# A two-block network kernel: the first block's in-projection, state space and attention in a new written-out order, its loads and its tail rearranged

## The chip, the cores and the metric

The kernel runs on one core of a Trainium2 chip. A core has five engines that work side by side and meet through semaphores: TensorE (PE, matrix products into the banks of PSUM), VectorE (DVE), ScalarE (ACT), GpSimd (POOL) and SyncE (SP, which here issues nearly all DMAs). Each engine takes its instructions strictly in the order in which they are written; a wait holds everything behind it on that engine. The metric is the device time of one execution in microseconds (us), lower is better.

## The reference

256 tokens of width 1024 go through one mixed block (the first) and two further layers. Only the first block's front half is touched by the change, so the rest is cut.

```python
def first_block(x, ...):
    u = rmsnorm(h, norm_mix[l])
    proj = u @ w_in[l]                                   # 1024 -> 2048
    u_ssm, q, k, v = jnp.split(proj, [D_SSM, D_SSM + D_ATTN, D_SSM + 2 * D_ATTN], axis=-1)
    y_ssm = s5_branch(u_ssm, A_re[l], A_im[l], log_dt[l], B_re[l], B_im[l], C_re[l], C_im[l],
                      D_skip[l], w_glu[l], b_glu[l])
    y_attn = stick_breaking_attention(q, k, v)           # 8 heads of 64
    gates = jax.nn.sigmoid((u @ w_gate[l] + b_gate[l]))  # 1024 -> 2048
    g_ssm, g_attn = jnp.split(gates, 2, axis=-1)
    merged = g_ssm * (y_ssm @ w_up_ssm[l]) + g_attn * (y_attn @ w_up_attn[l])
    h = h + merged @ w_out[l]
    hid = jax.nn.relu(rmsnorm(h, norm_mlp[l]) @ w_ff1[l])
    h = h + (hid * hid) @ w_ff2[l]

def s5_branch(...):    # 32 groups, 64 complex states each
    a_bar = jnp.exp(lam * dt);  b_bar = ((a_bar - 1.0) / lam) * B
    bu = b_bar @ u;  states = associative_scan(a_bar, bu)
    y = Re(C @ states) + D_skip * u
    y = jax.nn.gelu(y);  y = y * jax.nn.sigmoid(y @ w_glu + b_glu)

def stick_breaking_attention(q, k, v):
    z = (q @ k) * scale                                  # keys before the query only
    log_fail = log_sigmoid(-z);  after = cumsum from the right, without itself
    w = exp(log_sigmoid(z) + after);  out = w @ v
```

## The kernel before

**Slabs.** Every weight matrix is cut into slabs of 128 x 2048 words (1 MB), counted from 0 in `plan()`: 0 to 7 are the in-projection (two for the state space's input, two each for q, k and v), 8 to 15 the gates, 16 glu, 17 to 20 the up-projections, 21 to 24 the out-projection. There are three slots. A slab's way is: SP loads it into `raw` (L386) once VectorE has split the slab that was there; ScalarE rounds it into `wh` (`act_round`, L405), once PE has used the slot's former slab; VectorE makes the rest `wl` = raw - wh (`dve_split`, L412); PE multiplies three times, high by high, high by low, low by high (`mm3`, L445). A slab takes 48 such matmuls of 256 columns. Its result stands in bank 4 or 5 (slab's parity) until ScalarE evicts it (L1436 and L1440 to the SBUF tiles `us`, `qT`, `kT`, `v_tok`; L1445 with tanh for the gates), which gives `lin_free`.

**Start.** x comes in two token halves; `big_dve` and `big_act` make the norm, `big_pe` turns it (L688, with dummy products on zeros, `keep_clock`, L821, between and behind the halves), ScalarE scales it (L722), VectorE makes the two parts `uh` and `ul` (`big_parts`, L783 and L784), on which slab 0 waits. `b1_pe_start` turns small vectors (L1068, L1070), `b1_pe_vec2` those of the later layers (L1075), `b1_pe_params` the state-space factors (L1160, L1163).

**State space.** 16 tiles of 128 states. For each, `pe_bu` makes the input products in bank 0 or 1 (L1203, L1204: 32 rows of contraction, fp32), VectorE turns them by the phase, scans them and makes four products with sine and cosine (`dve_state`, L1228 to L1240, into `prod[s % 2]`), and `pe_y` multiplies these with four factor tiles (L1214) into 32 of the 128 rows of bank 3. So four tiles fill the bank, and `dve_y` (L1245) takes it. The phases come in four groups of four tiles: angles, rounded off, then sine and cosine on ScalarE (`act_phase`, L1193 to L1195). VectorE makes the angles of groups 0 and 1 (`dve_phase`, L1170 to L1173), GpSimd those of 2 and 3 (`pool_phase`, L1180 to L1185).

**Attention.** For each of 8 heads: scores (`pe_z`, L1260, L1261), softplus on ScalarE (`act_softplus`, L1291 to L1294, with table loads), sum and mask on GpSimd (L1045, L1034), suffix product on PE (`pe_tri`, L1267 to L1271), exp on ScalarE (`act_weights`, L1300), weighted sum on PE (`pe_av`, L1281, L1282). There is one buffer each for the softplus (`at_sp`) and the weights (`at_w`), and two banks of scores.

**What sets the order.** A loop over 16 steps g, one slab each, on PE, VectorE and ScalarE. The table `tiles_at` says which state tiles VectorE takes at a step; `pe_bu` of its first tile comes at the end of the step before, `pe_y` a step later; head h starts at step 8 + h:

```python
tiles_at = {5: [0], 6: [1], 7: [2, 3], 8: [4, 5], 9: [6, 7], 10: [8, 9], 11: [10, 11], 12: [12], 13: [13],
            14: [14, 15]}
PHASES_AT = {1: [0, 1], 5: [2], 11: [3]}
```

**Tail.** After the last head come gelu on ScalarE, its two parts, glu on PE (bank 0), a sigmoid, the product with y, its two parts, then the four up-projection slabs in the order attention, state space, attention, state space, each gated by VectorE (L1396), the sums, and the out-projection, whose end lets the next norm start.

Of the kernel before, what the change touches and what calls it, by code (L numbers as in the profile page):

```python
# [14 lines left out]
P = 128  # L15
# [60 lines left out]
KC1, KC2 = 8, 10  # L76
# [26 lines left out]
def plan():  # L103
# [25 lines left out]
    for n in range(8):  # L129
        add("gate1", n)  # L130
    mark("glu")
    add("glu", 0)
    mark("up1")
    for n, w in enumerate(("up_attn", "up_ssm", "up_attn", "up_ssm")):
        add(w, n // 2)
# [52 lines left out]
def hybrid_ssm_attention_kernel(nc, a, out):  # L188
# [14 lines left out]
    with ExitStack() as ctx:  # L203
# [27 lines left out]
        gates = sb("gates", [P, 2 * KD, T])  # L231
        shared = sb("shared", [P, 4096])
# [442 lines left out]
        def big_pe(pe, j):  # L675

            for tt in range(NTT):
                if tt == 1:
                    keep_clock(pe, KC1, CLOCK_BANK[j])
# [189 lines left out]
        rows_in = flat(act_out)  # L869
        b_nat = [gflat[:, 2048 + 256 * i:2304 + 256 * i].rearrange("p (s c) -> p s c", c=16) for i in range(2)]  # L870
# [11 lines left out]
        def phase(i, which):  # L882

            buf, at = ((shared, 0), (shared, 2048), (gflat, 2048), (shared, 0))[i]
            return buf[:, at + which * 1024:at + which * 1024 + 1024].rearrange("p (j t) -> p j t", j=4)
        prod = [small[:, i * 1024:(i + 1) * 1024].rearrange("p (a t) -> p a t", a=4) for i in range(2)]
        ATT = 3 * P
# [8 lines left out]
         ph_later, zeroed, gn_in, gn_t, vec2_in, vec2_t, w2_in, cd_in) = mk(  # L896
# [3 lines left out]
            "glu_y", "glu_h", "glu_l", "pair_read", "merged_sum", "merged_h", "merged_l", "ph_later", "zeroed", "gn_in", "gn_t", "vec2_in", "vec2_t", "w2_in",  # L900
            "cd_in")


        tiles_at = {5: [0], 6: [1], 7: [2, 3], 8: [4, 5], 9: [6, 7], 10: [8, 9], 11: [10, 11], 12: [12], 13: [13],
                    14: [14, 15]}
        PHASES_AT = {1: [0, 1], 5: [2], 11: [3]}
        NSTEP = 16
# [52 lines left out]
        def ssm_loads(sp):  # L960
            for i, nm in enumerate(("B_re", "B_im")):
                sp.dma_start(b_nat[i], a[nm][0].rearrange("(s g) p c -> (g p) s c", g=2)).then_inc(ssm_in, 16)
# [3 lines left out]
            sp.dma_start(steps_t[:, :], a["shape_tables"][:, 4 * T + 2 * P:]).then_inc(ssm_in, 16)  # L966

        def later_vectors(sp):

            for l in range(LAYERS):  # L970
                for name, r0 in ROW2.items():
# [1228 lines left out]
```

## Time and profile before

| | |
|---|---|
| median of 3 runs | 1687.04 us (1685.98 to 1690.28) |
| the profiled execution, its own time | 1686.85 us |
| its span, mean granted TensorE clock | 1685.1 us, 0.988 |
| PE busy | 1622.0 us (96%) |
| DVE, ACT, POOL busy | 1111.7 us (66%), 828.3 us (49%), 48.5 us (3%) |
| chain that ended last, by engine | PE 87%, DVE 8%, ACT 2%, SPq 1%, issue 1% |
| DMA | 264.53 MB, mean 157 GB/s |

"Busy" of PE counts overlapping matmuls once, with modelled ends; PE can be busy and yet slow, when the granted clock is below 1. The chain is followed back from the last instruction, at each step to what released it. Busy time of an engine off this chain costs nothing by itself.

### The profile page before, as it was taken

The page shows a single profiled execution, that of the slowest core. Times are in us where ns is not written, and L with a number is a line of the kernel's source. Part 1 is how long each engine was busy: PE and PEld are TensorE (multiplying, and loading weights), DVE is VectorE, ACT ScalarE, POOL GpSimd, SP SyncE. Part 2 cuts the span into 40 slices and gives each one's busy share as a digit, 9 for nine tenths or more (in the row PEclk, how much of TensorE's full clock was granted, in tenths as well). Part 3 has the DMA queues.
Part 4 walks back from the last instruction along what each step waited for, and adds up shares of the span by engine and source line. Part 5 has one row for each costly group of instructions (what it writes and reads, how often), then busy time and mean ns, then how long its engine had stood idle before and what let it go on. Part 6 is the DMA issues. An engine that isn't in the chain of part 4 may idle for free.

```text
span 1685.1 us, 24642 instructions
## 1 busy us (share of the span) xinstructions
PE 1622.0 (96%) x9690; PEld 1386.1 (82%) x9690; DVE 1111.7 (66%) x1480; ACT 828.3 (49%) x1077; POOL 48.5 (3%) x58
## 2 busy tenths in 40 slices
PE   5999899999999999999999999999999999999997
PEld 5876797888788888887888888788889877978886
DVE  5976766666766568865576655856577765666566
ACT  5545745343454346655454434634355655454443
POOL 1321100000000000000000000000000000000001
PEclk8999999999999999999999999999999999999999
DMA  7521243655655655532345556555664512454652
GB/s 206 153 72 51 101 143 122 197 184 189 215 175 174 199 199 147 178 101 76 126 150 175 181 192 208 168 173 188 211 193 132 175 51 101 150 171 155 207 190 100
DMA packets 206812, 264.53 MB, mean 157 GB/s; under 512 B 14106, under 2 KB 176276, under 8 KB 206740
## 3 DMA queue, kind: packets, MB, share of 16 engines
q1 hardware_dynamic: 206548, 263.50, 48.5%
q8 instruction: 49, 0.80, 0.2%
q14 instruction: 23, 0.19, 0.0%
q10 hardware_dynamic: 192, 0.04, 0.0%
HBM read 262.47 MB, written 1.05 MB: 156 GB/s over the span
## 4 chain that ended last, share of the span: by engine, by line
PE 87%; DVE 8%; ACT 2%; SPq 1%; issue 1%; DMA 0%; ACTq 0%; DVEq 0%
PE bank L445 41%; PE bank L479 21%; PE bank L483 11%; DVE wl L412 3%; PE bank L1621 2%; PE bank L1648 2%; PE bank L1214 1%; PE bank L1634 1%; ACT wh L405 1%; PE bank L688 1%; PE bank L821 1%; DVE wl L431 1%; PE bank L1649 1%; PE bank L1203 1%; DVE norm_small L740 1%
## 5 line engine op out<-in xcount | busy, mean ns | idle before, releaser
L412 DVE TENSOR_TENSOR wl<-raw,wh 128x2048 fp32r<-128x2048 f32 (+2 forms) x228 | 510.6, 2244 | 113.1 <-ACT wh L405 110.0
L405 ACT CAST wh<-raw 128x2048 fp32r<-128x2048 f32 (+3 forms) x235 | 437.6, 1866 | 90.3 <-PE bank L445 80.5
L479 PE MATMUL bank<-u_parts,wh 128*128 128x512 f32 x1664 | 424.1, 392 | 1.5 <-DVE u_parts L784 1.0
L479 PEld LDWEIGHTS bank<-u_parts,wh 128*128 128x128 f32 x1664 | 302.9, 188 | 59.6 <-issue 2.0
L445 PE MATMUL bank<-u_parts,wh 128*128 128x256 f32 (+1 forms) x1344 | 258.3, 293 | 9.0 <-ACT tmp L1436 7.1
L483 PEld LDWEIGHTS bank<-u_parts,wl 128*128 128x128 f32 x1664 | 231.2, 190 | 15.4
L483 PE MATMUL bank<-u_parts,wl 128*128 128x256 f32 x1664 | 243.1, 282 | 0.0
L445 PEld LDWEIGHTS bank<-u_parts,wh 128*128 128x128 f32 (+1 forms) x1344 | 212.9, 194 | 13.7 <-ACT tmp L1436 7.3
L445 PE MATMUL bank<-u_parts,wl 128*128 128x256 f32 (+1 forms) x672 | 192.6, 287 | 0.0
L445 PE MATMUL bank<-wh,hh 128*128 128x512 f32 x448 | 179.4, 400 | 7.1 <-DVE wl L412 5.1
L445 PE MATMUL bank<-wl,hh 128*128 128x512 f32 x448 | 175.6, 392 | 0.0
L445 PE MATMUL bank<-wh,hl 128*128 128x512 f32 x448 | 175.1, 391 | 0.0
L624 DVE TENSOR_TENSOR gates<-gates,bank 128x512 f32<-128x512 f32 x44 | 30.2, 687 | 189.3 <-ACT gates L588 189.3
L588 ACT COPY gates<-bank 128x512 f32<-128x512 f32 x44 | 25.8, 586 | 248.6 <-PE bank L483 248.6
L592 ACT COPY gates<-bank 128x512 f32<-128x512 f32 x60 | 35.2, 587 | 193.9 <-PE bank L483 193.9
L445 PEld LDWEIGHTS bank<-u_parts,wl 128*128 128x128 f32 (+1 forms) x672 | 130.4, 194 | 0.0
L445 PEld LDWEIGHTS bank<-wh,hh 128*128 128x128 f32 x448 | 84.5, 189 | 28.7 <-DVE wl L412 5.9
L445 PEld LDWEIGHTS bank<-wh,hl 128*128 128x128 f32 x448 | 84.5, 189 | 18.2
L445 PEld LDWEIGHTS bank<-wl,hh 128*128 128x128 f32 x448 | 84.5, 189 | 15.6
L445 PE MATMUL bank<-wh,u_parts 128*128 128x512 f32 (+1 forms) x320 | 83.8, 348 | 0.0
L613 DVE TENSOR_TENSOR gates<-gates,bank 128x512 f32<-128x512 f32 x60 | 41.2, 687 | 63.0 <-ACT gates L592 63.0
L445 PE MATMUL bank<-bh,wh 128*128 128x256 f32 x208 | 60.2, 289 | 6.9 <-DVE bl L1498 5.2
(340 smaller groups left out, 2030.5 us busy)
## 6 DMA issues: line engine op xcount, KB each, us to landing
raw<-ffn_wg SPq DMA_DIRECT2D x44, 1024.0 KB, 5.8
raw<-ffn_wu SPq DMA_DIRECT2D x44, 1024.0 KB, 5.4
raw<-ffn_wd SPq DMA_DIRECT2D x44, 1024.0 KB, 5.0
raw<-w_ff SPq DMA_DIRECT2D x32, 1024.0 KB, 5.2
raw<-w_in SPq DMA_DIRECT2D x28, 1024.0 KB, 5.5
raw<-w_out SPq DMA_DIRECT2D x12, 1024.0 KB, 5.0
raw<-w_gate SPq DMA_DIRECT2D x8, 1024.0 KB, 5.6
raw<-w_in SPq DMA_DIRECT2D x16, 512.0 KB, 5.3
```

The source lines that it names most:

```text
L405: ins = act.copy(dst, src)
L412: ins = dve.tensor_tensor(dst, src, upper.bitcast(F32), ALU.subtract)
L431: ins = dve.tensor_tensor(wl[:, slot, c], raw[:, slot, c], wh[:, slot, c].bitcast(F32), ALU.subtract)
L445: mm = pe.matmul(o, w, x, start=start and n == 0, stop=stop and n == 2, skip_group_check=True)
L479: return pe.matmul(two(bank[b + f]), slab_view(wh, slot, KD, WCOLS)[:, k, f * P:(f + 1) * P], u_parts[:, k, :, :], start=k == 0, stop=Fals ...
L483: return pe.matmul(bank[b + f][:, 0:T], slab_view(wl, slot, KD, WCOLS)[:, k, f * P:(f + 1) * P], uh[:, k, :], start=False, stop=k == KD - ...
L588: act.copy(up_z, halves(6)[1]).then_inc(up_half_out, 1)
L592: act.copy(gate_z, halves(4)[1]).then_inc(gate_half, 1)
L613: dve.tensor_tensor(gate_z, gate_z, halves(4)[0], ALU.add).then_inc(gate_sum, 1)
L624: dve.tensor_tensor(up_z, up_z, halves(6)[0], ALU.add).then_inc(up_sum, 1)
L1621: pe.matmul(b[:, c], q_(slice(tt * P, (tt + 1) * P)), k_(slice(0, (tt + 1) * P)), start=tt == 0, stop=True, skip_group_check=True)
L1648: pe.matmul(bank[6][r, 0:T], v_(0), pt[:, 0:T], start=first, stop=True, skip_group_check=True)
```

## The change

- **Order.** The loop is gone. `b1_pe`, `b1_act` and `b1_dve` are written out, step by step. PE takes most slabs in two halves (`pe_slab1(pe, g, half)`) with one to four small products between them. The state tiles start earlier (`pe_bu(0)` between the halves of slab 4, where it stood behind the whole slab 4), and so do the heads (scores of head 0 ahead of slab 6).
- **Output products in pairs.** `prod` has four buffers, two of them in a new tile `late_prod`; `pe_y(pe, s0)` takes tiles s0 and s0 + 1 and alternates between them, one factor after the other.
- **Phases.** ScalarE makes the angles (`act_turns`, 16 products with a column), VectorE rounds them off for all four groups; GpSimd has none. ScalarE also takes over the copies of the diagonal factors (`b1_act_diag`) and of the output factors (`b1_act_turned`). The phases of groups 2 and 3 stand in the buffers of 0 and 1.
- **Loads.** On SP, slabs 0 to 2 come first, then the steps, C and B_re, slab 3, B_im, slab 4; the vectors of the later layers in three parts ahead of slabs 6, 7 and 8, the small weights ahead of slab 12.
- **Start.** 20 dummy products before the first transposes, `b1_pe_start` between the two token halves in place of 8 dummies.
- **Tail.** Slab 16 is now the first attention up-projection, 17 glu (banks 2 and 3), 18 the second attention one, 19 and 20 those of the state space. `dve_up` is split into `dve_gate` and `dve_merge`.
- The DMA scratch is set to 1024, which makes room for `late_prod`.

```diff
-KC1, KC2 = 8, 10
+KC0, KC1, KC2 = 20, 8, 10
...
-                if n == 1:
-                    ssm_loads(sp)
-                if n == 2:
-                    later_vectors(sp)
+                if n == 3:
+                    steps_and_c(sp)
+                    b_load(sp, 0)
+                if n == 4:
+                    b_load(sp, 1)
+                if n in (6, 7, 8):
+                    later_vectors(sp, n - 6)
+                if n == 12:
+                    cmp_weights(sp)
                 sp_slab(sp, n)
...
+        def pe_y(pe, s0):
+            if s0 % 4 == 0 and s0 >= 4:
+                pe.wait_ge(y_taken, s0 // 4)
+            pe.wait_ge(prod_done, s0 + 2)
             for n, (c, q) in enumerate(((0, 0), (1, 3), (2, 2), (2, 1))):
-                mm = pe.matmul(bank[3][32 * j:32 * j + 32, 0:T], c_t[c][:, s, :], p[:, q, :], start=n == 0, stop=n == 3)
-            mm.then_inc(y_done, 1)
+                for s in (s0, s0 + 1):
+                    j = s % 4
+                    mm = pe.matmul(bank[3][32 * j:32 * j + 32, 0:T], c_t[c][:, s, :], prod[s % 4][:, q, :], start=n == 0, stop=n == 3)
+                    if n == 3:
+                        mm.then_inc(y_done, 1)
...
-            if s >= 2:
-                dve.wait_ge(y_done, s - 1)
-            p = prod[s % 2]
+            if s >= 4:
+                dve.wait_ge(y_done, s - 3)
+            p = prod[s % 4]
...
+        def act_turns(act, i):
+            s = phase(i, 1)
+            if i < 2:
+                act.wait_ge(ssm_in, 16 * 7)
+            else:
+                act.wait_ge(prod_done, 4 * (i - 1))
+            for j in range(4):
+                ins = act.activation(s[:, j, :], steps_t[:, :], ACT.Identity, scale=col(TURNS)[:, 4 * i + j:4 * i + j + 1])
+            ins.then_inc(ph_in, 1)
...
+            pe_slab1(pe, 3)
+            b1_pe_params(pe)
+            pe_slab1(pe, 4, 0)
+            pe_bu(pe, 0)
+            pe_slab1(pe, 4, 1)
+            b1_pe_vec2(pe)
+            pe_slab1(pe, 5, 0)
+            pe_bu(pe, 1)
+            pe_slab1(pe, 5, 1)
+            pe_bu(pe, 2)
+            pe_z(pe, 0)
+            pe_slab1(pe, 6, 0)
...
+            pe_slab1(pe, 9, 0)
+            pe_bu(pe, 6)
+            pe_y(pe, 2)
+            pe_tri(pe, 1)
+            pe_slab1(pe, 9, 1)
+            pe_bu(pe, 7)
+            pe_av(pe, 1)
+            pe_z(pe, 2)
...
+            pe_slab1(pe, 15, 1)
+            pe_av(pe, 7)
+            pe_y(pe, 14)
+            pe.wait_ge(o_taken, 4)
+            pe.wait_ge(bu_free, ST)
+            lin_pe(pe, N_UP1, 0, None, KS, 512, 4, *upper(KS))
             pe.wait_ge(gelu_l, 1)
-            lin_pe(pe, N_GLU, 0, None, KS, DS, 4, lambda k: bh[:, k, :], lambda k: bl[:, k, :])
+            pe.wait_ge(w_exp, HEADS)
+            lin_pe(pe, N_GLU, 2, None, KS, DS, 4, *upper(0))
```

SP, from its first DMA on. `raw<-w_in` is a slab, `res<-x` a token half, the others state-space parameters and vectors. Before:

```order
L985 DMA res<-x 128x1024 x2
L386 DMA raw<-w_in 128x8x256
L962 DMA gates<-B_re 128x16x16
L962 DMA gates<-B_im 128x16x16
L965 DMA hid<-C_re 128x4x64 x2
L965 DMA stat<-C_im 128x4x64 x2
L966 DMA steps_t<-shape_tables 128x256
L386 DMA raw<-w_in 128x8x256
L977 DMA act_out<-ln_f_g 8x128
```

And now:

```order
L989 DMA res<-x 128x1024 x2
L389 DMA raw<-w_in 128x8x256 x3
L963 DMA steps_t<-shape_tables 128x256
L966 DMA hid<-C_re 128x4x64 x2
L966 DMA stat<-C_im 128x4x64 x2
L969 DMA gates<-B_re 128x16x16
L389 DMA raw<-w_in 128x8x256
L969 DMA gates<-B_im 128x16x16
L389 DMA raw<-w_in 128x8x256 x2
```

Three slabs stand ahead of the parameters, where one did; the vectors have gone behind slab 5.

PE, between the slabs of step 8 and step 9 before, around the output products of tiles 2 and 3 (L1214; L1203 and L1204 are `pe_bu`):

```order
L1203 MATMUL bank<-tmp,tables 128x256
L1204 MATMUL bank<-tmp,tables 128x256
L1267 MATMUL bank<-small,suffix 128x256
L1268 MATMUL bank<-small,minus1 128x128
L1269 MATMUL bank<-small,suffix 128x128
L1271 MATMUL bank<-earlier,identb 128x128 x2
L1214 MATMUL bank<-small,tables 32x256 x8
L1203 MATMUL bank<-tmp,tables 128x256
L1204 MATMUL bank<-tmp,tables 128x256
L1260 MATMUL bank<-sq 128x256
L1261 MATMUL bank<-sq 128x128
```

Now, between the halves of slab 9, the same two tiles (L1221 is `pe_bu`, L1234 `pe_y`, L1290 to L1294 `pe_tri`):

```order
L1221 MATMUL bank<-tmp,tables 128x256 x2
L1234 MATMUL bank<-late_prod,tables 32x256 x8
L1290 MATMUL bank<-small,suffix 128x256
L1291 MATMUL bank<-small,minus1 128x128
L1292 MATMUL bank<-small,suffix 128x128
L1294 MATMUL bank<-earlier,identb 128x128 x2
```

Before, two state products and a head's scores stood with them, and the second `pe_bu` needed a bank that VectorE frees after `dve_y`; now it is one group less, and the next `pe_bu` stands behind half a slab.

VectorE, at the end of the heads (L1245 is `dve_y`, L1308 the last head's low part, L412 a split, L1498 gelu's low part, L1396 the gating). Before:

```order
L1308 TENSOR_TENSOR bl<-bank,bh 128x256
L412 TENSOR_TENSOR wl<-raw,wh 128x2048
L1245 SCALAR_TENSOR_TENSOR tmp<-tmp,vec1,bank 128x256
L1308 TENSOR_TENSOR bl<-bank,bh 128x256
L1498 TENSOR_TENSOR bl<-tmp,bh 128x1024
L412 TENSOR_TENSOR wl<-raw,wh 128x2048
L1501 TENSOR_TENSOR tmp<-tmp,small 128x1024
```

And now (L1334, L1266, L415, L1695, L1496 in the same roles):

```order
L415 TENSOR_TENSOR wl<-raw,wh 128x2048
L1334 TENSOR_TENSOR bl<-bank,bh 128x256
L1266 SCALAR_TENSOR_TENSOR tmp<-tmp,vec1,bank 128x256
L415 TENSOR_TENSOR wl<-raw,wh 128x2048 x2
L1695 TENSOR_TENSOR bl<-tmp,bh 128x1024
L1496 SCALAR_TENSOR_TENSOR small<-gates,bank 128x512 x2
L1698 TENSOR_TENSOR tmp<-tmp,small 128x1024
```

Two splits now stand between `dve_y` and gelu's low part; the second of them is of slab 18, which ScalarE rounds behind gelu.

## Rows read from the trace of the kernel before

**Rows 1.** The page, part 1: busy us, share of span, instructions.
```profile
PE 1622.0 (96%) x9690; PEld 1386.1 (82%) x9690; DVE 1111.7 (66%) x1480; ACT 828.3 (49%) x1077; POOL 48.5 (3%) x58
```
**Rows 2.** Busy by stretch: length, engines (instructions), granted clock, DMA share, GB/s.
```profile
6.00:8.00 2.00, 0.00 (x0) 0.00 (x0) 1.60 (x5) 1.73 (x4) 1.18 (x4) 1.00 1.09 376
...
60.00:204.00 144.00, 135.05 (x851) 108.08 (x850) 108.43 (x149) 79.62 (x100) 31.63 (x24) 0.95 0.28 90
```
**Rows 3.** PE in order of time: start, busy, instruction [idle before, releaser].
```profile
16.75 0.47 PE L445 MATMUL bank<-u_parts,wh 128*128 128x256 f32 x2
...
36.62 0.80 PE L445 MATMUL bank<-u_parts,wh 128*128 128x256 f32 x2 [7.10 <-ACT tmp L1436]
...
51.95 1.09 PE L1160 MATMUL bank<-ident,gates 128*128 128x128 f32 x8 [1.00 <-DVE gates L1139]
...
103.15 0.69 PE L1203 MATMUL bank<-tmp,tables 32*128 32x256 f32 x2 [3.97 <-DVE hid L1229]
...
265.60 1.24 PE L688 MATMUL bank<-ident,sq 128*128 128x128 f32 x8 [1.05 <-ACT sq L706]
```
**Rows 4.** VectorE and ScalarE in order of time, the start.
```profile
11.52 2.29 DVE L412 TENSOR_TENSOR wl<-raw,wh 128x2048 fp32r<-128x2048 f32 x1 [0.25 <-ACT wh L405]
15.85 0.29 DVE L783 CAST u_parts<-tmp 128x256 fp32r<-128x256 f32 x1 [2.04 <-ACT tmp L722]
...
15.34 2.49 ACT L722 ACTIVATE tmp<-bank,vec 128x256 f32<-128x256 f32 x6 [3.86 <-PE bank L688]
...
32.25 1.90 ACT L405 CAST wh<-raw 128x2048 fp32r<-128x2048 f32 x1 [9.75 <-DMA raw<-w_in]
```
**Rows 5.** SP's queue in order of time: start, us issuing, DMAs.
```profile
2.81 6.00 SPq L962 DMA_DIRECT2D gates<-B_im  x1
...
26.57 28.04 SPq L386 DMA_DIRECT2D raw<-w_in  x6
```
**Rows 6.** The chain that ended last, in order of time: start, us, piece.
```profile
61.66 5.94 PE bank L445 x48
...
74.61 1.84 PE bank L1214 x8
...
96.44 2.75 PE bank L1214 x16
...
99.61 2.28 DVE wl L412
...
106.05 8.04 PE bank L445 x48
...
140.51 7.90 PE bank L445 x48
```
**Rows 7.** L1214 on PE by tenths of a microsecond (in brackets: records in flight).
```profile
97.40:97.50 0.10, 0.10 (x5) 1.00 0.00 0
...
75.00:75.10 0.10, 0.10 (x2) 1.00 0.00 0
```
**Rows 8.** The chain again, from the last head to glu.
```profile
202.42 0.50 ACT small L1300
...
203.61 0.23 PE bank L1282 x2
...
204.26 1.28 ACT L1456
...
207.71 1.24 DVE bl L1498
...
209.00 7.84 PE bank L445 x48
```
**Rows 9.** VectorE in order of time: first state tile, and two tiles in a row.
```profile
65.43 0.69 DVE L1228 TENSOR_TENSOR act_out<-bank,shared 128x512 f32<-128x512 f32 x1
...
101.81 0.68 DVE L1228 TENSOR_TENSOR act_out<-bank,shared 128x512 f32<-128x512 f32 x1
...
106.62 0.69 DVE L1228 TENSOR_TENSOR act_out<-bank,shared 128x512 f32<-128x512 f32 x1
```

More of the change, by code:

```diff
@@ L130, in plan @@
         add("gate1", n)
+    mark("up1")
+    add("up_attn", 0)
     mark("glu")
     add("glu", 0)
[L133 to L135 removed]
+    add("up_attn", 1)
+    add("up_ssm", 0)
+    add("up_ssm", 1)
     mark("out1")
@@ L1277, in pe_av @@
             pe.wait_ge(w_exp, h + 1)
+            if h == 0:
+                for b_ in range(2):
+                    pe.wait_ge(lin_free[b_], 4)
             if h % 2 == 0 and j >= 1:
@@ new lines, in dve_up, with act_evict @@
+        def dve_up(dve, n0, r, q):
+            p = q // 2
+            dve_gate(dve, n0 + q, 2 * (q % 2), "AB"[q % 2], p, merged[:, 4 * p:4 * p + 4, :] if q % 2 == 0 else gated)
+            if q % 2:
+                dve_merge(dve, r, p, q + 1)
+        def act_evict(act, g):
+            wait_used(act, N_IN1 + g)
+            b = bank[4 + g % 2]
+            if g < 2:
+                act.copy(us[:, 2 * g:2 * g + 2, :], two(b)).then_inc(lin_free[g % 2], 1)
+            elif g < 8:
+                o = (qT[:, 2 * (g - 2):2 * (g - 2) + 2, :] if g < 4 else kT[:, 2 * (g - 4):2 * (g - 4) + 2, :] if g < 6
+                     else v_tok[:, :, (g - 6) * WCOLS:(g - 5) * WCOLS])
+                act.activation(o, two(b), ACT.Copy, scale=SCALE_N if g < 4 else 1.0).then_inc(lin_free[g % 2], 1)
+            else:
+                for f in range(2):
+                    k = 2 * (g - 8) + f
+                    ins = act.activation(gates[:, k, :], b[:, f * T:(f + 1) * T], ACT.Tanh, scale=0.5, bias=half_b[:, k:k + 1])
+                ins.then_inc(lin_free[g % 2], 1)
@@ new lines, in b1_dve @@
+            dve_state(dve, 5)
+            dve_split(dve, 10)
+            dve_state(dve, 6)
+            dve_y(dve, 0)
+            dve_split(dve, 11)
+            dve_phase(dve, 2)
+            dve_split(dve, 12)
+            dve_state(dve, 7)
+            dve_state(dve, 8)
+            dve_state(dve, 9)
+            dve_o(dve, 0)
+            dve_split(dve, 13)
+            dve_split(dve, 14)
+            dve_state(dve, 10)
+            dve_y(dve, 1)
+            dve_phase(dve, 3)
+            dve_state(dve, 11)
@@ L1495, in b1_dve @@
+            dve_state(dve, 12)
+            dve_o(dve, 1)
+            dve_split(dve, 15)
+            dve_state(dve, 13)
+            dve_y(dve, 2)
+            dve_state(dve, 14)
+            dve_o(dve, 2)
+            dve_state(dve, 15)
+            dve_split(dve, N_UP1)
+            dve_o(dve, 3)
             dve_y(dve, 3)
-            dve_o(dve, 3)
+            dve_split(dve, N_GLU)
+            dve_split(dve, N_UP1 + 2)
+            for b in range(2):
+                dve.wait_ge(lin_free[b], 8)
```

475 lines of the change are left out of this document (277 added, 198 removed).

## The prediction, made before the changed kernel had run

> **What bounds the kernel now.** I read the page first. TensorE (PE) is busy 96% of the span [rows 1], so time can come only from where it idles, runs at its low clock, or does dearer work than needed. The changed stage is the first 265 us; nothing after it is edited, so its end (the last matmul of the out-projection at 264.6, ahead of the 1.05 us wait at 265.60 [rows 3]) is the mark: what that moves, the kernel moves. The busy time of 60 to 204 us shows that something is lost in the middle of it: granted clock 0.95 and 135 of 144 us busy [rows 2]. Then I follow the start in order of time [rows 3 to 5], and the chain of work that ended last [rows 6, 8]. Four losses are seen there.
>
> A: PE idles 7.10 us ahead of its third slab (36.62), because ScalarE waited 9.75 us for that slab's load [rows 3, 4]; SP issued it at 26.57, behind seven parameter DMAs and 32 vector and small-weight DMAs [rows 5]. The slab then starts at the low clock: its first pair of matmuls is busy 0.80 us, where slab 0's took 0.47 at 16.75 [rows 3], and its first nine groups of three take 0.64 us each instead of 0.36, some 2.2 us of loss until 42.3.
> B: PE waits 3.97 us at 103.15 [rows 3] for VectorE, which does `dve_y`, then a split of 2.28 us, and only then frees the bank of the next state tile; afterwards the clock is low, and the slab takes 8.04 us against 5.94. A second such wait ends at 136.65, with a slab of 7.90 [rows 6].
> C: a tile's four output products take 1.84 us, two tiles in a row 2.75 [rows 6].
> D: from 203.84 to 209.00 PE waits for gelu, and the glu slab takes 7.84 [rows 8].
>
> **The change, part by part,** against this execution (1686.85 us, its span 1685.1; the median of the runs shown is 1687.04, so the two agree).
>
> 1. Start. Twenty dummies come before anything else, and the vector transposes move between the two token halves. Before, ScalarE gets its first turned half at 15.34 [rows 4]. Now the vector transposes wait for the vectors as before (10.2), but the first token half is turned by then and the second follows near 11.7. VectorE, whose first split ends at 13.81 [rows 4], becomes the bound: its parts start at 13.85 instead of 15.85, slab 0 at 14.7 instead of 16.75. Gain 2.0 us.
>
> 2. Loads. SP issues slabs 0, 1 and 2 at once, then steps, C and B_re, slab 3, B_im, slab 4. x and three slabs are 4 MB; at the 376 GB/s of 6 to 8 us [rows 2] they are in by about 14 us. Splits 1 and 2 follow the parts on VectorE, 2.25 us each: to 21.4 and 23.7. PE starts slab 1 at 21.4 and slab 2 at 27.3, where it was 36.62: 9.3 earlier, 2.0 of it item 1's. The low clock of 36.6 to 42.3 goes too, 2.2 us. Gain 7.3 + 2.2 = 9.5. What is late next is ScalarE's queue: slab 1's eviction at 27.9, eight products for phases 0 and 1 (3.3 us, at the 0.415 us of a 128x256 row: six in 2.49 [rows 4]), rounds of 1.9, the diagonal copies until 37.1, and PE wants them at 39.2; the output factors are copied at 43.4, wanted at 44.2; slab 3's eviction at 47.4, wanted at 48.5. These are margins of 2.1, 0.8 and 1.1 us. PE's wait of 1.00 at the parameter transposes [rows 3] goes, with two shorter ones of 0.6 together: gain 1.6; for the thin margins I take 1.0 back.
>
> 3. Loss B. The first state tile starts on VectorE near 46.7 instead of 65.43, and a tile takes it 4.7 us (101.81 to 106.62 with a gap) [rows 9]; from there it is one to four tiles ahead of PE. I walked the queues with durations of this trace (half a slab 2.97, state product 1.06, output pair 2.0, scores 0.84, suffix product 1.15, weighted sum 0.80): bu(7) is wanted at 94 and its bank free at 89, bu(14) wanted at 153 and free at 146. The suffix products wait for ScalarE's softplus and GpSimd; the least margins are 1.7 us, at heads 3 and 7. So both stalls go, 3.97 each, and the slow groups behind them (slab 2.1, state product, scores and weighted sum 1.0): gain 2 x 7.07 = 14.1. Phases off GpSimd: GpSimd is waited for less, no gain on the path. ScalarE takes 16 products (6.6 us), some copies (4 us) and one more table load (1.28 [rows 8]); it is then busy some 111 of 155 us, hidden by PE's work as long as the order fits, and 1.28 to 2 us for each place where it doesn't.
>
> 4. Loss C. Six pairs at 2.75 and four single tiles at 1.84 are 23.9 us. In a pair up to 5 records are in flight together, in a single tile 2 [rows 7]: the second tile's column strip works beside the first. Interleaved, each strip has its 8 records at 0.23, so 1.84 and one step, say 2.0; eight pairs 16.0, gain 7.9. Bounds: 1.84 (gain 9.2), and no more overlap than now (2.75, 22.0, gain 1.9). I take 2.0, as the stretch with both strips runs each at its full rate.
> The Trainium skill, page "TensorE: Matmul & The Clock Gate", section "Part 3: Packing small matmuls", says that a weight load overlaps a running matmul only where the row groups differ; these products all use all 128 rows. By that rule the interleaved records would take turns, which is the third rival's time. The five records in flight speak against it.
>
> 5. Slabs in halves. 48 matmuls at the 0.12 us of an undisturbed slab are 5.76; with a group of another shape behind it a slab takes 5.94 [rows 6], so a return costs 0.18. There are 8 more returns: loss 1.5.
> The Trainium skill, page "TensorEngine Tiling (Array Packing)", section "Key Properties", says that changing the tiling mode drains the engine, which speaks against cutting slabs. The 0.18 us is what the trace shows of it.
>
> 6. Last heads. Two short waits for ScalarE around 202.42 [rows 8] go, as the weighted sums have slack now: gain 1.0.
>
> 7. Tail. Before, from 203.84 to 264.6 are 60.7 us. Now the first up slab (5.94) runs while gelu is made. The last output pair ends near 169.5. ScalarE has the glu slab's round and the table load until 172, gelu and its copy until 174.1 (204.26 to 207.71 are 3.45 with the load [rows 8]), then the round of the third up slab until 176.0; VectorE stands at that slab's split, until 178.2, and only then makes gelu's low part, 1.24 [rows 8]: 179.5. PE is through the up slab at 175.5, so it still waits 4.0 us, and I charge 2.0 for the clock as behind the 3.97 us waits. glu ends at 187.4; three up slabs, the zeroing and the out-projection take 40.3: 227.7. That is 58.2 us, gain 2.5. Bounds: 0 if the wait is 6 us, 4.5 if the clock holds.
>
> Sum: 2.0 + 9.5 + 1.6 - 1.0 + 14.1 + 7.9 - 1.5 + 1.0 + 2.5 = 36.1, and 1686.85 - 36.1 = 1650.8. In one line: PE starts slab 0 at 14.7, has 154.6 us of work and waits to the last pair (169.3), and ends the stage near 227.7, 36.9 earlier, 35.9 with the margins' 1.0. I predict 1651.
>
> **Rivals.** First: the order fits worse than my walk, and two waits are long enough to drop the clock. One costs what loss B does, 7.1 us, two 14.2: 1665. For it: margins of 0.8 to 2.1 us at five places, ScalarE strictly in order. Against: VectorE's lead.
> Second: slab 2 is still late, as the queue doesn't deliver three slabs in a row at that rate, or slab 3, behind the small-element loads. The 9.5 stays away: 1660. For it: SP was held 6.00 us at B_im [rows 5]. Against: slabs 1 and 2 are ahead of those loads now.
> Third: the output records take turns. 16 at 0.23 are 3.7 a pair, 29.4 in all, 5.5 more than before instead of 7.9 less: 1664. With today's overlap only, 1657.
> Fourth, the other side: **the head chain becomes the bound.** One buffer each for the softplus and the weights ties a head's suffix product to ScalarE's place in line; where the new order puts rounds, phases and table loads ahead of a head's softplus, PE stops at that product. At 7.1 us a stop with its clock, the 36.1 are gone with the sixth of eight heads, and all eight cost 56.8: 1651 + 57 = 1708. Against: ScalarE is about 72% loaded.
> That the change doesn't do what it says: the phases' leaving GpSimd frees no PE time, which I already count at nothing.
>
> **How the numbers follow.** Forecast 1651, with 1645 to 1657 from the bounds of items 4 and 7: 0.60. First rival 0.18, second 0.07, third 0.11 (0.04 of it at 1664), fourth 0.03, something else 0.01. The range 1645 to 1666 takes in the second and third and most of the first's single and double stops; left out are the rest of the first (0.06), the fourth, and the forecast's own ends (0.08): 0.17. Faster by over 0.3% (about what a measurement of this kernel can tell from no change; below 1682) is every case but the fourth and a sliver: 0.96; within 0.3% 0.015, slower 0.025.
>
> **What would show it.** Slab 2 starting near 27; the first state tile on VectorE near 47; no PE wait for a state bank and a granted clock of 1.00 from 20 to 170; output pairs of 16 records in about 2.0 us, the last ending near 169; one wait of about 4 us before glu; the next norm's transposes near 229. Wrong would be: PE waits at suffix products (first, fourth), pairs over 2.7 us (third), a round that waits for a load (second).

## The result, and the profile after

The changed kernel takes 1650.93 us (median of 4 runs, 1650.58 to 1651.91), the kernel before 1687.3 us in the same session: a ratio of 0.9777, 95% interval 0.9765 to 0.9789. The forecast was 1651 with a range of 1645 to 1666. The profiled execution has a span of 1648.4 us where it was 1685.1. Its page: the span and part 1 [the counterparts of rows 1], and from part 2 the granted clock, in tenths, over 40 equal slices:

```profile
span 1648.4 us, 24663 instructions
PE 1608.8 (98%) x9702; PEld 1378.8 (84%) x9702; DVE 1107.4 (67%) x1466; ACT 839.5 (51%) x1104; POOL 25.6 (2%) x46
PEclk9999999999999999999999999999999999999998
```

PE's busy time hardly differs (1622.0 before): it idles less, and at the low clock it also counts as busy. What PE waited for from the start to 226 us, then stretches of that time with the columns of [rows 2]:

```profile
PE bank L826 <- POOL cvalid L1032: 4.9, 1, 4.9
PE bank L448 <- DVE bl L1695: 3.9, 1, 3.9
PE bank L448 <- DVE u_parts L789: 2.3, 1, 2.3
PE bank L448 <- DVE bl L1701: 0.2, 1, 0.2
```

```profile
15.00:19.00 4.00, 4.00 (x23) 4.00 (x22) 3.79 (x13) 3.43 (x6) 0.00 (x0) 0.57 1.03 151
19.00:23.00 4.00, 4.00 (x36) 4.00 (x35) 4.00 (x3) 3.20 (x3) 0.00 (x0) 1.00 1.08 280
...
177.00:183.00 6.00, 5.97 (x29) 5.97 (x30) 1.17 (x2) 0.00 (x0) 0.00 (x0) 0.53 0.46 174
...
20.00:170.00 150.00, 150.00 (x1101) 128.37 (x1100) 131.78 (x191) 112.74 (x151) 14.57 (x16) 1.00 0.40 121
```

From 20 to 170 us PE is busy all the time at the full clock; before, 60 to 204 us had 135 busy of 144 at 0.95 [rows 2]. The four losses of the prediction are answered one by one. A: the wait of 7.10 us ahead of the third slab [rows 3] is gone; PE goes through slabs 0 to 3 until the parameter transposes at 39.3. B: both state-bank waits are gone. C: the output pairs, in the chain of work that ended last (start, us, piece), where a pair of tiles took 2.75 and a single one 1.84 [rows 6]:

```profile
73.34 1.85 PE bank L1234 x16
...
157.77 1.85 PE bank L1234 x16
```

D: there is still one wait of 3.91 ahead of glu, and the clock is low behind it (0.53 from 177 to 183 us). PE's waits in order of time, then the chain around it [answers to rows 3 and 8]:

```profile
14.69 0.48 PE L448 MATMUL bank<-u_parts,wh 128*128 128x256 f32 x2 [2.25 <-DVE u_parts L789]
177.03 0.58 PE L448 MATMUL bank<-bh,wh 128*128 128x256 f32 x1 [3.91 <-DVE bl L1695]
192.40 0.38 PE L448 MATMUL bank<-bh,wh 128*128 128x256 f32 x1 [0.19 <-DVE bl L1701]
227.00 1.24 PE L693 MATMUL bank<-ident,sq 128*128 128x128 f32 x8 [1.04 <-ACT sq L711]
```

```profile
166.47 1.79 ACT wh L408
168.28 1.28 ACT L1613
169.57 1.07 ACT tmp L1613
...
171.62 1.91 ACT wh L408
173.55 0.06 DVE wl L415
...
175.76 1.23 DVE bl L1695
176.99 0.04 issue
177.03 8.47 PE bank L448 x48
```

ScalarE has gelu's high part ready near 171.7. VectorE stands at the split of slab 18 instead, for which ScalarE first rounds the slab, and comes to gelu's low part at 175.8. PE has been idle since 173.1. The mark that the prediction chose, the transposes of the next norm, moved from 265.60 [rows 3] to 227.00.

### The profile page after: what moved, and what is told of

The parts are those of the page before. It is cut to its first block, busy times and chain, and to the rows that moved or that the text cites. A ratio compares the mean times of both kernels' runs of the same rounds, so it can differ in the third digit from the quotient of the medians.

```text
span 1648.4 us, 24663 instructions
## 1 busy us (share of the span) xinstructions
PE 1608.8 (98%) x9702; PEld 1378.8 (84%) x9702; DVE 1107.4 (67%) x1466; ACT 839.5 (51%) x1104; POOL 25.6 (2%) x46
## 4 chain that ended last, share of the span: by engine, by line
PE 89%; DVE 7%; ACT 3%; issue 1%; DMA 0%; ACTq 0%; DVEq 0%
PE bank L448 43%; PE bank L482 21%; PE bank L486 11%; DVE wl L415 2%; PE bank L1822 2%; PE bank L1849 2%; ACT wh L408 1%; PE bank L1221 1%; PE bank L1835 1%; PE bank L693 1%; PE bank L1234 1%; DVE norm_small L745 1%; PE bank L826 1%; DVE wl L434 1%; PE bank L1850 1%
## 5 line engine op out<-in xcount | busy, mean ns | idle before, releaser
L415 DVE TENSOR_TENSOR wl<-raw,wh 128x2048 fp32r<-128x2048 f32 (+2 forms) x228 | 509.7, 2240 | 99.8 <-ACT wh L408 96.8
L448 PE MATMUL bank<-u_parts,wh 128*128 128x256 f32 (+1 forms) x1344 | 254.1, 290 | 3.1 <-DVE u_parts L789 2.3
L486 PEld LDWEIGHTS bank<-u_parts,wl 128*128 128x128 f32 x1664 | 231.2, 190 | 15.4
L448 PEld LDWEIGHTS bank<-u_parts,wh 128*128 128x128 f32 (+1 forms) x1344 | 208.6, 191 | 9.0 <-issue 4.7
```

The lines of the kernel that those rows point to most:

```text
L415: ins = dve.tensor_tensor(dst, src, upper.bitcast(F32), ALU.subtract)
L448: mm = pe.matmul(o, w, x, start=start and n == 0, stop=stop and n == 2, skip_group_check=True)
L486: return pe.matmul(bank[b + f][:, 0:T], slab_view(wl, slot, KD, WCOLS)[:, k, f * P:(f + 1) * P], uh[:, k, :], start=False, stop=k == KD - ...
```

## A thing to know before the experiments: the untouched rest is not constant

The mark moved by 38.6 us, the span only by 36.7. From the mark to the end the two kernels execute the same instructions with the same waits (one of them 0.3 us longer), in 1419.5 us before and 1421.4 after. Of these 1.9 us 1.5 lie in one stretch: from a norm's transposes to a wait of PE in the second block, 76.8 us before and 78.3 after. Inside it stand four rotary products of 32x32 by 512 columns in a row (L1936, eight records, 3.62 us), and here is what the granted clock does behind them, first before, then after:

```profile
704.00:707.00 3.00, 3.00 (x27) 1.51 (x26) 2.80 (x5) 0.33 (x1) 0.00 (x0) 1.00 1.09 373
707.00:710.00 3.00, 3.00 (x36) 2.68 (x34) 2.97 (x2) 1.19 (x2) 0.00 (x0) 1.00 0.75 232
```

```profile
665.00:668.00 3.00, 3.00 (x14) 1.19 (x13) 2.80 (x5) 0.82 (x1) 0.00 (x0) 0.88 1.07 368
668.00:671.00 3.00, 3.00 (x33) 3.00 (x31) 2.94 (x3) 0.00 (x0) 0.00 (x0) 0.55 0.89 281
```

There is a second such place. Some 179 us behind the mark PE waits 2.02 us in every kernel, and in 10 of the 14 executions below the clock is low right behind it, which costs 1.1 us (not in the runs 3, 5, 9 and 11). The two places together account for nearly all of the differences in the column "rest".

So the experiments are read by places inside the first 230 us, and the medians beside them. "Rest" is the span less the mark; ratios are to the kernel before in the same session (its medians: 1687.3, 1687.9 for the runs 1 to 4, 1688.7 for 5 to 8, 1689.6 for 9 to 12).

| run | median us | ratio, 95% | glu starts | mark | rest |
|---|---|---|---|---|---|
| before | 1687.3 | 1 | 209.00 | 265.60 | 1419.5 |
| changed kernel | 1650.93 | 0.9777 (0.9765 to 0.9789) | 177.03 | 227.00 | 1421.4 |
| 1 tile by tile | 1655.48 | 0.9803 (0.9786 to 0.9819) | 183.01 | 230.54 | 1422.8 |
| 2 loads late | 1660.09 | 0.9829 (0.9813 to 0.9846) | 188.86 | 237.89 | 1422.7 |
| 3 before, y step late | 1676.31 | 0.9931 (0.9914 to 0.9947) | 195.48 | 251.49 | 1421.5 |
| 4 gelu first | 1644.02 | 0.9735 (0.9719 to 0.9751) | no wait | 220.86 | 1423.1 |
| 5 tail filled | 1648.27 | 0.9755 (0.9739 to 0.9771) | 176.81 | 224.36 | 1421.5 |
| 6 start filled | 1650.26 | 0.9765 (0.9749 to 0.9782) | 176.87 | 225.91 | 1423.0 |
| 7 slabs whole | 1651.07 | 0.9774 (0.9758 to 0.9791) | 178.88 | 227.77 | 1419.7 |
| 8 phases on GpSimd | 1649.74 | 0.9766 (0.9749 to 0.9782) | 177.22 | 226.07 | 1419.6 |
| 9 rotary products spread | 1649.35 | 0.9764 (0.9751 to 0.9778) | 177.25 | 226.12 | 1420.1 |
| 10 three edits | 1643.55 | 0.9726 (0.9713 to 0.9740) | no wait | 220.20 | 1421.1 |
| 11 and five slabs whole | 1641.13 | 0.9716 (0.9703 to 0.9730) | no wait | 218.77 | 1420.1 |
| 12 no start dummies | 1651.43 | 0.9766 (0.9753 to 0.9779) | 176.79 | 226.55 | 1423.0 |

## Experiments

**1. The pairs, tile after tile.**

```diff
-            for n, (c, q) in enumerate(((0, 0), (1, 3), (2, 2), (2, 1))):
-                for s in (s0, s0 + 1):
+            for s in (s0, s0 + 1):
+                for n, (c, q) in enumerate(((0, 0), (1, 3), (2, 2), (2, 1))):
```

> The changed kernel, in which the eight output products of a pair are written tile after tile again (order of the two loops in pe_y exchanged); all else stays, the four product buffers and the places of the pairs too. Theory of item 4 (two column strips work beside each other only when their records alternate): each of the eight pairs goes from the 1.85 us of the changed kernel's trace back to about 2.75, +0.9 x 8 = +7.2, so about 1658, with no new wait. Rival (the strips overlap however they are ordered, and the gain of the pairs came from bringing two tiles together): 1651, pairs still at 1.85. Rival (pairs longer by 0.9 us push a later product past its slack): 1662 or more, with a wait of PE that the changed kernel doesn't have.

Measured: every pair takes 2.74, as expected, but the median is 1655.5 where 1658 was. Two rows of its chain, and its wait ahead of glu:

```profile
73.13 2.74 PE bank L1234 x16
...
162.88 2.74 PE bank L1234 x16
```

```profile
183.01 0.39 PE L448 MATMUL bank<-bh,wh 128*128 128x256 f32 x1 [3.02 <-DVE bl L1695]
```

So alternating the two column strips is worth 0.89 a pair, 7.1 in all (in the order of this run the second tile's records start only with the first tile's fifth of eight, at 73.95, and half of each tile runs alone), and bringing tiles into pairs the remaining 2.0 of the 9.1 (23.9 to 14.8). But the mark is only 3.5 later than the changed kernel's, and the ratio only 0.0026 (4.4 us) higher: PE reaches the gelu wait 6.9 later, the low part comes 6.0 later, the wait is 0.9 shorter, and behind it the clock doesn't fall (glu to slab 19 takes 12.9 us instead of 15.4). Slab 0 happened to run at the full clock too (slab 2 starts at 27.55 instead of 27.77). 7.1 - 0.9 - 2.4 - 0.2 = 3.6, and 3.5 are measured. So 3.3 of the pairs' 7.1 was lost again at the tail's wait in the profiled executions; 2.4 of it is the clock's part, which varies (run 5), and by the ratios 2.7 was lost.

**2. The old order of SP.**

```diff
-                if n == 3:
-                    steps_and_c(sp)
-                    b_load(sp, 0)
...
+                if n == 1:
+                    b_load(sp, 0)
+                    b_load(sp, 1)
+                    steps_and_c(sp)
+                if n == 2:
+                    for part in range(3):
+                        later_vectors(sp, part)
+                    cmp_weights(sp)
```

> The changed kernel with SP's order of before: slab 0, the seven parameter loads, slab 1, all 24 later vectors and the eight small weights, slab 2. All other engines keep the changed order. Theory of item 2: slab 2 starts near 36.6 us on PE instead of 27.9, PE sits idle some 7 to 9 us ahead of it and then runs some groups at the low clock (2.2 us by the trace of before): +9 to +11, so 1660 to 1662. Rival (the engines' new orders take the loads' place: the gain of the start came from the order of ScalarE and VectorE, not from the loads): within 2 us of 1651. Rival (the parameter path, which the early loads no longer feed late, becomes faster and gives part back): 1655 to 1658.

Measured: slab 1 starts 1.8 later (23.83, behind a new wait of 1.51 for VectorE's split), slab 2 at 37.22, and its first pair of matmuls runs at the low clock (0.77 us):

```profile
37.22 0.77 PE L448 MATMUL bank<-u_parts,wh 128*128 128x256 f32 x2 [7.37 <-ACT tmp L1521]
```

Slab 3, and glu too, start 11.8 later (45.36 instead of 33.53, 188.86 instead of 177.03); the mark is 10.9 later, as the clock's fall behind the tail's same wait of 3.91 cost 1.0 less in this execution; the ratio is 0.0052 (8.8 us) higher. One more wait appears, of 0.2 us at the start's vectors. The loads' place, and not the engines' new order, gives the start its gain; between slab 3 and glu nothing of it was given back.

**3. Loss B alone, in the kernel before.**

```diff
-                for s in tiles_at.get(g - 1, []):
-                    if s % 4 == 3 and s < ST - 1:
-                        dve_y(dve, s // 4)
                 if g >= 4:
                     dve_split(dve, n + 2)
                 for s in tiles_at.get(g, []):
                     dve_state(dve, s)
+                for s in tiles_at.get(g - 1, []):
+                    if s % 4 == 3 and s < ST - 1:
+                        dve_y(dve, s // 4)
```

> The kernel before with one edit: on VectorE the y step of the tiles of slab g-1 is written behind the split and the states of slab g instead of ahead of them, so that VectorE no longer stands at it while the next state tile's bank is waited for. Theory of loss B: both 3.97 us waits of PE for that bank go, and the low clock behind each (3.1) with them: 1687.3 - 14.1 = 1673. If only the waits go and the clock falls in any case: 1679. Rival (the order of VectorE only moves the wait: the split or the state's products are late next): 1683 to 1690, with PE waits at another product.

Measured: in place of the two 3.97 us waits there are two short ones, and the clock holds. PE in order of time, then 60 to 160 us of this kernel:

```profile
111.29 0.69 PE L1203 MATMUL bank<-tmp,tables 32*128 32x256 f32 x2 [0.25 <-DVE hid L1229]
125.94 0.69 PE L1203 MATMUL bank<-tmp,tables 32*128 32x256 f32 x2 [0.97 <-DVE hid L1229]
```

```profile
60.00:110.00 50.00, 50.00 (x340) 41.25 (x339) 43.85 (x56) 26.39 (x30) 19.33 (x11) 1.00 0.36 113
110.00:160.00 50.00, 48.53 (x318) 38.16 (x316) 44.82 (x64) 34.16 (x44) 9.80 (x9) 1.00 0.26 85
```

From slab 2 to glu PE needs 159.8 us instead of 172.4, 12.6 less: 6.7 of waits (7.94 less 1.22) and 5.9 of clock, 2.9 for each, where I charged 3.1. The median falls by 11.6, where 14.1 was expected. One moved step of 0.48 us gives nearly all of item 3; only the last 1.2 us of waits are left to the written-out order. The rival (the wait moves elsewhere) falls.

**4. Gelu's low part ahead of the split of slab 18** (changed kernel, VectorE).

```diff
             dve_split(dve, N_GLU)
-            dve_split(dve, N_UP1 + 2)
-            for b in range(2):
-                dve.wait_ge(lin_free[b], 8)
             dve.wait_ge(gelu_h, 1)
             dve.tensor_tensor(bl[:, 0:KS, :], us[:, :, :], bh[:, 0:KS, :].bitcast(F32), ALU.subtract).then_inc(gelu_l, 1)
+            dve_split(dve, N_UP1 + 2)
+            for b in range(2):
+                dve.wait_ge(lin_free[b], 8)
```

> The changed kernel with one edit: on VectorE the low part of gelu is written ahead of the split of slab 18 instead of behind it. ScalarE has gelu's high part ready at 171.7 in the changed kernel's trace, so the low part ends near 172.9, and PE is through the first up slab at 173.1. Theory of item 7: PE's wait of 3.9 us ahead of glu goes, and with it the low clock of 176 to 183 (about 2.5 us): 1651 - 6.4 = 1644.5. If the clock falls there in any case: 1647. Rival (the split of slab 18 or glu's own chain of sigmoid, product and parts is next, and takes it back): 1649 to 1651, with a PE wait at slab 18 or at slab 19.

Measured: the first up slab and glu are one piece of 96 matmuls in the chain, at 5.94 a slab:

```profile
167.47 11.88 PE bank L448 x96
179.35 0.02 issue
179.38 0.03 ACT small L1618
```

The mark is 6.1 earlier, the ratio 0.0042 (7.1 us) lower, with intervals apart: 1644.0 us. The cause of the tail's wait is shown: not gelu, but VectorE's place in line. The next wait, 0.20 for the gated product's low part, is the same as before.

**5. The same gap, filled.**

```diff
-            pe.wait_ge(gelu_l, 1)
             pe.wait_ge(w_exp, HEADS)
+            keep_clock(pe, 26, 7)
+            pe.wait_ge(gelu_l, 1)
```

> The changed kernel with 26 dummy products (128x256, 0.144 us each in the start's rows) into a free bank between the first up slab and the wait ahead of glu: 3.7 us of work in the 3.9 us gap, the wait itself stays. Theory (the gap costs its length plus a clock that falls because of it): only the low clock of 176 to 183 goes, glu's slab takes 5.9 instead of 8.5: 1651 - 2.4 = 1648.5. Rival (the clock falls there for another reason): 1651. Rival (the dummies run past the end of the wait): up to 1652.

Measured: glu starts at the same time, but the clock holds:

```profile
176.81 0.39 PE L448 MATMUL bank<-bh,wh 128*128 128x256 f32 x1 [0.81 <-DVE bl L1696]
189.75 0.39 PE L448 MATMUL bank<-bh,wh 128*128 128x256 f32 x1 [0.20 <-DVE bl L1702]
```

12.9 us between the two rows, and 15.4 in the changed kernel: the gap costs its 3.9 us and 2.4 of clock, and dummies save the second part. That is read from the traces; the intervals of the two ratios overlap. The seven executions that kept a wait of 3.6 us or more ahead of glu need 14.2 to 15.4, so the clock's part is 1.3 to 2.4. Behind waits of 3.02 and 0.81 it was nothing.

**6. The gap ahead of slab 0, filled** with `keep_clock(pe, 15, 5)` ahead of `pe_slab1(pe, 0)`.

> The changed kernel with 15 dummy products more just ahead of slab 0, in PE's 2.25 us gap from 12.4 to 14.7. Theory (the gap lowers the clock for slab 0, groups of three at 0.64 us from 15.6 to 18.7): slab 0 runs at the full clock, but it is fed by VectorE's parts, one in 0.66 us until 19.1, and slab 1's split ends at 21.4; slab 0 ends near 20.4 instead of 22.1, PE waits for slab 1 until 21.4: gain 0.7, 1650.2. Rival (the clock falls there whatever stands before): 1651. What would be larger than 1.5 us speaks against both.

Measured: no wait before slab 0, slab 1 at 21.75, behind a wait of 0.77 for VectorE's split:

```profile
21.75 0.50 PE L448 MATMUL bank<-u_parts,wh 128*128 128x256 f32 x2 [0.77 <-DVE wl L415]
```

That is 0.3 earlier than the changed kernel's 22.01, and 0.7 was expected: the bound is VectorE's split, as told, but it lets slab 1 start at 21.75 and not at 21.4. The median can't tell it. The low clock of 15 to 19 us costs only this much. It isn't in every execution: slab 0 ran at the full clock in the runs 1, 5 and 12, behind gaps of 1.29, 1.36 and 2.00 us, and at the low one behind gaps of 1.97 to 2.53 (runs 2, 4, 7, 8, 9 and the changed kernel).

**12. No dummies at the start** (the line `keep_clock(pe, KC0, 5)` taken out).

> The changed kernel without the 20 dummy products at the very start (4.86 to 9.1 us). The transposes of the first token half start when x is normalised, not when the dummies end, and VectorE's split of slab 0 (11.6 to 13.8) stands ahead of the parts in either case. If the dummies are there for the clock of the start: transposes at the low clock, slab 0 wholly at the low clock, up to 3 us more at slab 1, which VectorE's split (21.4) lets start no earlier: 1651 to 1653. If the clock is low in slab 0 anyway, as in the changed kernel's trace: 1651, no change.

Measured: the first transposes take 1.94 us, where they took 1.03. Their records start 0.21 us apart instead of 0.11, the step of a low clock; the trace has no record of the clock itself before 11.15 us, so that is worked out and not read:

```profile
7.92 1.94 PE L693 MATMUL bank<-ident,sq 128*128 128x128 f32 x8 [7.92 <-ACT sq L711]
14.91 0.48 PE L448 MATMUL bank<-u_parts,wh 128*128 128x256 f32 x2 [2.00 <-DVE u_parts L789]
```

Slab 0 starts within 0.22 of the changed kernel's all the same and ran at the full clock. The 20 dummies buy nothing that can be measured.

**7. All cut slabs whole** (the ten calls `pe_slab1(pe, g, 0)` become `pe_slab1(pe, g)`, the ten second halves go).

> The changed kernel with the ten cut slabs (4 to 6 and 9 to 15) whole again, each at the place of its first half; every other step of every engine keeps its order. Theory of item 5: each cut costs a return of 0.18 us (two halves take 3.06 and 2.92 in the changed kernel's trace, a whole slab 5.76 to 5.94), gain 10 x 0.15 = 1.5 if nothing is late; but what stood between the halves now comes 2.9 us later, and a state tile, a suffix product or an eviction that had less slack than that makes PE wait. If the halves are there for the waits, the loss is larger than 1.5: 1652 to 1660 with PE waits at state, score or suffix products. If they aren't needed: 1649.5.

Measured: 1651.07, no change, but for two reasons against each other. There are four new waits, 0.64, 0.86, 0.58 and 0.22 us, at the scores of heads 5 and 7, at the last weighted sum and at the first up slab. Behind the second one the clock falls:

```profile
150.56 0.70 PE L1283 MATMUL bank<-sq 64*128 64x256 f32 x2 [0.86 <-ACT small L1326]
```

```profile
150.00:154.00 4.00, 3.44 (x11) 2.28 (x12) 3.90 (x8) 3.39 (x6) 0.00 (x0) 0.66 0.00 0
154.00:158.00 4.00, 4.00 (x33) 3.99 (x32) 0.79 (x2) 2.87 (x5) 0.00 (x0) 0.91 0.00 0
```

Glu starts 1.85 later. So some of the cuts hold off the waits of the later heads. Together they pay for themselves and no more, as far as these medians tell.

**8. Phases 2 and 3 on GpSimd again.**

```diff
-            act_turns(act, 2)
-            act_turns(act, 3)
-            dve_phase(dve, 2)
-            dve_phase(dve, 3)
...
+                for i, step in {0: [(2, 0)], 1: [(2, 1), (2, 2)], 2: [(3, 0)], 3: [(3, 1)], 4: [(3, 2)]}.get(h, []):
+                    pool_phase(pool, i, step)
```

> The changed kernel with phases 2 and 3 on GpSimd again (products, rounding and subtraction, spread behind heads 0 to 4); ScalarE and VectorE lose those eight products and four rounding steps. Theory of item 3 (the phases are off the path, whoever does them): within 1.5 us of 1651, with VectorE's steps a little longer where GpSimd works beside it. Rival (GpSimd is slow at them, 13 us a phase by the trace of before, and its head steps come late, or phase 2 itself does): PE waits at suffix products or at state tile 8, and loses 4 to 14 us with the clock: 1655 to 1665.

Measured: 1649.74, glu at 177.22 (177.03), no new wait of PE. GpSimd's steps for the two phases, from the groups of instructions (busy us, mean ns):

```profile
L1209 POOL TENSOR_SCALAR shared<-steps_t,cols 128x256 f32<-128x256 f32 x8 | 8.4, 1070 | 10.5 <-DVE late_prod L1276 10.5
L1212 POOL TENSOR_SCALAR shared<-shared 128x1024 f32<-128x1024 f32 x2 | 7.6, 3820 | 0.0
L1214 POOL TENSOR_TENSOR shared<-shared 128x1024 f32<-128x1024 f32 x2 | 5.5, 2740 | 0.1
```

21.5 us of GpSimd's time, none of it on the path. Taking the phases off it, which the change does, is worth nothing by itself.

**9. The rotary products spread**, one ahead of the 48 small products that follow them and one behind each of the first three quarters of these, in both layers.

```diff
+                    if between is not None and k in (3, 7, 11):
+                        between((k + 1) // 4)
...
-            for b in range(4):
+            def rope_perm(b):
                 pe.wait_ge(m_read, 4 * l + b + 1)
                 pe.matmul(bank[b][HD:QK_M, :], perm_m[HD:QK_M, HD:QK_M], qm[HD:QK_M, 2 * b:2 * b + 2, :], start=True,
                           stop=True).then_inc(m_perm, 1)
+            rope_perm(0)
             pe.wait_ge(bank7_free, B7 * l + NROPE + 1)
-            cmp_hidden(1)
+            cmp_hidden(1, rope_perm)
```

> The changed kernel with one edit far behind the changed stage, in both layers of the second block: the four rotary products of 32x32 by 512 columns, which stand in a row in 3.6 us and use a sixteenth of the array, are spread through the 48 small products of the second compression slab (one ahead, one behind each quarter). What is to be explained: with the same instructions and the same waits, the time from the first transposes behind the changed stage to the end of the kernel is 1419.5 us in three executions and 1421.4 to 1423.0 in seven; all of the difference lies in the stretch of these products in each layer (76.8, 78.3 or 79.8 us), where the granted clock falls to 0.50 for some 3 or 6 us with PE busy throughout. Theory (four products in a row that use so little of the array lower the clock in some executions): spread, both stretches take 76.8, and the time from that mark to the end is 1419.5; the median falls by 1 to 2 us, 1649 to 1650. Rival (the clock falls there for another reason, the matmuls of 30 rows on either side among them): stretches of 78.3 or 79.8 are still found, and the median stays at 1651. Rival (a rotary step is late for VectorE now): the stretch takes longer without a low clock.

Measured: the clock holds.

```profile
664.00:668.00 4.00, 4.00 (x30) 1.73 (x28) 1.38 (x2) 0.00 (x0) 0.00 (x0) 1.00 1.09 361
668.00:672.00 4.00, 4.00 (x31) 3.21 (x31) 3.76 (x3) 3.00 (x4) 0.00 (x0) 1.00 0.15 47
```

With the products in a row, 12 of 22 such stretches (11 executions, two layers) took 78.2 to 78.3 or 79.7 to 79.8 us, the others 76.8; spread, all six (runs 9, 10 and 11) took 77.4 to 77.5. So the four in a row bring the falls about. Whether that is for their shape, as the theory has it, or for something else about them isn't separated here. The edit has a price that I had not foreseen, 0.65 us a stretch against an undisturbed 76.8, with more changes of shape on PE, and so it saves little: 1.0 on average less 0.65. Most of the 2.2 us by which run 9's ratio lies under the changed kernel's isn't from it, and the intervals overlap: the profiled execution's rest is 1.3 us shorter than the changed kernel's, and 1.1 of that is the fall at the second place, 179 us behind the mark, which it was spared. That the median came out as forecast is luck.

**10. The edits of 4, 6 and 9 together.**

> Three edits of the experiments together on the changed kernel: the low part of gelu ahead of the split of slab 18, the 15 dummies ahead of slab 0, the rotary products spread. From the medians of the runs so far: 1644.0 with the first, 0.5 to 0.7 for the second, 1 to 2 for the third, so 1642 (1640.5 to 1643.5). If the clock's falls at the start and in the second block are not tied to these places, 1644.

Measured 1643.55, just above the expected 1640.5 to 1643.5; the mark is 6.8 us earlier than the changed kernel's. The intervals of this run and of run 4 (0.9719 to 0.9751) overlap, so what the two other edits add to run 4's isn't told by the medians; in the profiled executions the mark is 0.7 earlier and the rest 1.9 shorter.

**11. And slabs 4, 5, 6, 9 and 10 whole.**

> As the kernel with the three edits, and slabs 4, 5, 6, 9 and 10 whole again, the ones ahead of which the run with all slabs whole showed no wait. Five returns of 0.15 to 0.18 us: 0.8 us less than the kernel with the three edits if no wait appears. If a wait appears that the later heads' order had hidden: same or longer.

Measured 1641.13: no wait appears, and the mark is 1.43 earlier than in run 10, where 0.8 was expected. In the chain, first of run 10 and then of run 11, the first half of slab 10 takes 3.06 (the second one too) and the whole slab 5.93:

```profile
95.21 3.06 PE bank L448 x24
```

```profile
93.95 5.93 PE bank L448 x48
```

Five cuts cost 0.3 us each. This is the fastest version, 0.6% under the changed kernel by the ratios (0.9716 and 0.9777, intervals apart).

## Why the prediction came out, point by point

The four losses, their causes and most of their prices were right. That the time was right within 0.1 us is partly luck: the stage ended 1.7 us earlier than I had it (225.96, not 227.7), and the rest took 1.9 us longer, by low clocks that I had not counted. **The step that failed** is the first paragraph's "what that moves, the kernel moves": the rest of the kernel varies between 1419.5 and 1423.1 us with the same instructions.

- Item 1, the start: slab 0 at 14.69, forecast 14.7. That it would run at the low clock was missed; PE reached slab 1 at 22.0 instead of 21.4. Run 6 gets 0.3 of it back.
- Item 2, the loads: slab 2 at 27.8, forecast 27.3; run 2 puts their worth at 11.8 at glu, where items of 9.5 and 1.6 less 1.0 stood. One term was summed too low: the third slab took 8.41 us before and 5.76 now, 2.65 and not the 2.2 charged for its low clock. The first state tile starts on VectorE at 47.15, forecast 46.7; the waits at the parameters are gone, and the margins held. The second rival (slab 2 or 3 late) was close for slab 3 alone: ScalarE waited 0.86 us for its load, VectorE 0.51 for that round, and PE for neither.
- Item 3, loss B: 14.1 forecast; run 3 gives 12.6 with 1.2 of waits left.
- Item 4, the pairs: 2.0 a pair taken, 1.85 measured, at the lower bound of 1.84; gain 9.1 instead of 7.9. The reason was right: the records start two by two, one of each strip, 0.007 us apart, and the twos follow each other at 0.216, the step at which a single tile's records follow too. The step for "one more record" was not needed. Four records are in flight at a time, first in the changed kernel; in run 1, where the first of two tiles runs alone, it is two [as rows 7]:

```profile
73.53:73.72 0.19, 0.19 (x4) 0.10 (x2) 1.00 0.09 9
```

```profile
73.50:73.60 0.10, 0.10 (x2) 0.09 (x1) 1.00 0.08 18
```

  The Trainium skill, page "TensorE: Matmul & The Clock Gate", section "Part 3: Packing small matmuls", lets a weight load overlap a running matmul only where the row groups differ. These all use 128 rows, each matmul record is busy 0.379 (with a modelled end), and the weight loads, 0.11 each, start just behind the start of a matmul record and not behind its end: this trace doesn't agree with the rule. The third rival falls by the 1.85 us alone.
- Item 5, the cuts: I charged 0.18 for each of eight; run 11 shows 0.3 for each of five. Mis-sized by the count and by the price.
- Item 6, the last heads: the trace of before shows one wait there, of 0.64 us, and none is left; 1.0 was forecast.
- Item 7, the tail: the wait was 3.91 (forecast 4.0), the place and the reason as told, and the clock's price 2.4 (forecast 2.0; it is 1.3 to 2.4 in other executions). What I missed is that the pairs' gain runs against this wait (run 1): items 4 and 7 aren't independent.
- The last pair starts at 165.2 and PE is free for the up slab at 167.1, 2.2 earlier than forecast; 1.2 of it are the pairs, the other 1.0 I didn't trace.
- First and fourth rival: no PE wait from 20 to 170 us. Run 7 shows that they weren't idle: with ten halves merged, waits at scores appear and one of them lowers the clock, but each costs 0.2 to 0.9 us and one fall of the clock, not 7.1.

## What to carry to other kernels

Where small matmuls write to different column strips, alternate the strips record by record; side by side in program order isn't enough (2.74 against 1.85 us). Before adding up gains, look for the next wait that another engine sets: up to half of the pairs' gain vanished at the gelu wait, and one VectorE instruction moved past a split was worth more (7 us). And time a small edit by marks inside the trace: far from the edit the same instructions took up to 3.5 us more or less.

## What the runs showed of the hardware

The granted clock fell to its lower level (0.50, that is 1.2 of 2.4 GHz) with PE busy throughout, behind 3.6 us of 32x32 products, in 12 of 22 passes through them, and in none of 6 once they were spread. The Trainium skill, page "TensorE: Matmul & The Clock Gate", section "HAM oscillation — how this bites in real kernels", lays such falls to gaps in which PE is idle; here there was no gap, so the rule doesn't cover this case. An idle time of 0.86 us among products of 64 rows was followed by a fall (run 7), one of 3.02 us between whole slabs was not (run 1): the length of a gap alone doesn't decide. Whether what stands around it does, or chance, isn't settled, for the same place differs between executions too: behind 2.0 us ahead of slab 0 the clock fell in the runs 2, 8 and 9 and not in run 12 (which lacks the dummies at the start), and behind the 2.02 us some 179 us past the mark in 10 of 14. The same gap of 3.9 us cost 1.3 to 2.4 us of clock from one execution to the next.
